# The opening of a two-block kernel: the first tile turned as loaded, its norm row as a column, the first weights by halves

## The chip, the cores and the metric

The kernel runs on one core of a Trainium2 chip. A core has a matrix engine (TensorE, "PE" in the profile), VectorE (DVE), ScalarE (ACT), GpSimd (POOL) and SyncE (SP), each with its own instruction stream; they wait for each other on semaphores. Transfers from HBM are asked for by an engine's queue (SP and ACT here by hardware queues, POOL by a software one) and moved by 16 DMA engines. The metric is the device time of one launch in microseconds, the median of several.

## The reference

Two transformer blocks of two layers each, on 256 tokens of width 1024, in float32. The change touches only how the first layer starts:

```python
for i in range(DEPTH):
    h = rms_norm(x, norm_mix_pre[i])
    z = h @ w_in[i]
    c_q, c_kv, k_rope, q_c, k_c, v_c, g_a, g_b, g_c = jnp.split(z, split_points, axis=-1)
    ...

def rms_norm(x, gain):
    y = x * lax.rsqrt(jnp.mean(x * x, axis=-1, keepdims=True) + RMS_EPS)
    return y * gain
```

The scale of a token (the rsqrt) is a factor of its row and can be applied behind the product with the weights; the gain is a factor of a column of `x` and has to be applied ahead of it. Positions of the tokens feed a rotation of some columns and a mask by distance for windowed attention.

## The kernel before

**Tiles.** The 256 tokens are two tiles of 128 rows: `xs[:, 0]` (x0) and `xs[:, 1]` (x1). A matmul needs the activations with the width on the partitions, so each tile is multiplied by its gain row into `ht` (VectorE, "h" in the profile), turned by TensorE against `ident` in two groups of four 128x128 blocks into PSUM banks 2 and 3, and copied out.

**Two parts.** Each factor is kept as a high part rounded to the fast matmul type and a low part, the rest. ScalarE makes `act_hi` from the turned tile and `whi` from the loaded weights `raw`; VectorE makes `act_lo` and `wlo` by subtraction. A product is three passes: high rows by high weights (L571), low rows by high weights (L565), high rows by low weights (L556).

**Units.** The weights stream through three slots in units of up to 128x2048 words (1 MB), each loaded by two transfers. SyncE asks for unit u as soon as the low part of unit u - 3 is made. The first product takes its 512 columns from units 0 and 1 (tile 0, then tile 1), the second from units 2 and 3. A product of a unit with one tile is 12 matmuls of 512 columns. `stay_warm(n)` is n turns of `ident` whose result nobody reads; at the start 18 of them stand behind the turns of tile 0.

**Order.** All is written by hand, engine by engine, and every engine does its instructions in order. In the opening ScalarE first asks for the gain row (broadcast to all partitions), the positions (`posk` along the free axis for all partitions, `posq` down the partitions) and the rotation tables. It squares x0, makes `act_hi`, then the halves of unit 0 (`first_split`, counted by `s_first_hi` and `hi`), asks for x1, and does the halves of unit 1. VectorE has the gain product of tile 0, `act_lo`, the low parts of both units, the gain product of tile 1, then the work on positions (6 steps, `PART_STEPS`) and distances (8 more) for `mask`, then `act_lo` of tile 1 and the low part of unit 2. GpSimd makes constants, the inverse root of tile 0, and a table of angles from `posq`. TensorE turns tile 1 in the middle of the pass by low weights of unit 1. Then each engine enters the loop over the two layers, whose body begins with the first product; `Ready` holds what a product waits for at the seam. Semaphores named in `counted` are raised to `BASE` by TensorE at the start.

## Time and profile before

| | us |
|---|---|
| median of 3 runs (1907.06 to 1907.66) | 1907.35 |
| span of the profiled execution | 1904.2 |
| around the span, if that execution took the median time | 3.15 |
| TensorE busy | 1868.7 |
| VectorE, ScalarE, GpSimd busy | 1107.1, 958.9, 150.4 |
| first product's first matmul begins | 13.03 |
| unit 3's first matmul begins | 29.84 |

The profiler shows the span, from the first to the last instruction; no time of its own is given for that execution beside it, so the median stands for it. Times of the opening are counted from the span's start. A timeline row is a run of like instructions: start, time from the first's start to the last's end, how many, and in brackets how long the engine had stood idle and what released it. Ends of matmuls are modelled and overlap with the next, so starts are to be compared.

### The profile page before, as it was taken

To read this page: it belongs to the slowest core of one execution; us is meant where nothing else is said; L and a number is where in the kernel's file an instruction comes from. 1 tells how busy PE (TensorE), PEld (TensorE's weight loads), DVE (VectorE), ACT (ScalarE), POOL (GpSimd) and SP (SyncE) were. 2 spreads that over 40 slices of the span, in tenths; PEclk is the share of its full clock that TensorE was granted. 3 is DMA by queue.
4 is the path that set the end of the run, shared out by engine and by line. 5 is a ranking of instruction groups with operands and counts; after the bars stand their busy time and mean duration, and the time that the engine had idled before them with its cause. 6 is when DMAs were issued, how large, how long until landed. Compare 5 with 4: busy or idle time off the path is not lost.

```text
span 1904.2 us, 26150 instructions
## 1 busy us (share of the span) xinstructions
PE 1868.7 (98%) x8988; PEld 1523.3 (80%) x8988; DVE 1107.1 (58%) x1365; ACT 958.9 (50%) x1277; POOL 150.4 (8%) x259
## 2 busy tenths in 40 slices
PE   8999999999999999999999999999999999999998
PEld 7777888887877888888788887788888888868887
DVE  6666565448676575446754456655465445575454
ACT  5664454445675464445544446644454444564443
POOL 5210010001300010000100012000011000100000
PEclk9999999999999999999999999999999999999999
DMA  6335565554524546565655554455565564526553
GB/s 225 123 119 184 179 217 190 178 183 151 166 90 166 205 164 204 193 198 177 201 190 178 179 202 141 143 195 179 182 219 170 184 198 169 195 90 197 178 178 107
DMA packets 204987, 332.72 MB, mean 175 GB/s; under 512 B 11360, under 2 KB 150240, under 8 KB 204896
## 3 DMA queue, kind: packets, MB, share of 16 engines
q1 hardware_dynamic: 200240, 319.08, 49.9%
q0 software_dynamic: 3120, 11.02, 1.7%
q10 hardware_dynamic: 1536, 1.47, 0.2%
q8 instruction: 50, 0.82, 0.2%
q14 instruction: 41, 0.34, 0.1%
HBM read 330.48 MB, written 1.05 MB: 174 GB/s over the span
## 4 chain that ended last, share of the span: by engine, by line
PE 88%; issue 4%; DVE 3%; ACT 3%; DMA 1%; POOL 0%; DVEq 0%; SPq 0%; POOLq 0%; ACTq 0%
PE ps L571 27%; PE ps L565 27%; PE ps L556 27%; PE ps L598 3%; ACT whi L1254 1%; PE ps L771 1%; PE ps L759 1%; PE ps L787 1%; ACT prob L1352 1%; DVE wlo L1738 1%; DMA raw<-w_in_dram 0%; DVE prob L1878 0%; DMA xs<-x_dram 0%; DVE prob L1851 0%; DVE act_lo L1744 0%
## 5 line engine op out<-in xcount | busy, mean ns | idle before, releaser
L1738 DVE TENSOR_TENSOR wlo<-raw,whi 128x2048 fp32r<-128x2048 f32 (+1 forms) x306 | 690.6, 2257 | 510.3 <-ACT whi L1254 509.8
L1254 ACT ACTIVATE whi<-raw 128x2048 fp32r<-128x2048 f32 (+1 forms) x306 | 576.9, 1885 | 422.4 <-PE ps L565 422.3
L571 PE MATMUL ps<-whi,act_hi 128*128 128x512 f32 (+2 forms) x1632 | 442.0, 392 | 5.1 <-issue 2.4
L556 PE MATMUL ps<-wlo,act_hi 128*128 128x512 f32 (+2 forms) x1632 | 438.7, 387 | 0.0
L565 PE MATMUL ps<-whi,act_lo 128*128 128x512 f32 (+2 forms) x1632 | 432.2, 386 | 1.5 <-DVE act_lo L1744 1.5
L565 PEld LDWEIGHTS ps<-whi,act_lo 128*128 128x128 f32 x1632 | 303.9, 188 | 64.4 <-DVE act_lo L1744 2.3
L556 PEld LDWEIGHTS ps<-wlo,act_hi 128*128 128x128 f32 x1632 | 302.2, 188 | 61.8 <-issue 1.1
L571 PEld LDWEIGHTS ps<-whi,act_hi 128*128 128x128 f32 x1632 | 297.5, 188 | 64.1 <-issue 2.8
L1299 ACT ACTIVATE hid<-ps,stat 128x256 f32<-128x256 f32 x132 | 62.6, 474 | 282.9 <-PE ps L598 197.4
L2320 POOL TENSOR_TENSOR stat<-stat,eps 128x1 f32<-128x1 f32 x43 | 22.4, 521 | 1471.4 <-ACT prob L1286 1471.1
L1791 DVE SCALAR_TENSOR_TENSOR hid<-ps,stat,hid 128x256 f32<-128x256 f32 x132 | 63.6, 482 | 123.7 <-ACT hid L1299 123.7
L571 PE MATMUL ps<-whi,hid_hi 128*128 128x512 f32 x496 | 133.2, 390 | 0.0
L556 PE MATMUL ps<-wlo,hid_hi 128*128 128x512 f32 x496 | 133.1, 390 | 0.0
L565 PE MATMUL ps<-whi,hid_lo 128*128 128x512 f32 x496 | 132.6, 389 | 0.0
L565 PEld LDWEIGHTS ps<-whi,hid_lo 128*128 128x128 f32 x496 | 93.1, 188 | 19.3
L556 PEld LDWEIGHTS ps<-wlo,hid_hi 128*128 128x128 f32 x496 | 93.0, 188 | 19.3
L571 PEld LDWEIGHTS ps<-whi,hid_hi 128*128 128x128 f32 x496 | 92.7, 188 | 18.9
L1352 ACT ACTIVATE prob<-prob,soft 128x128 f32<-128x128 f32 (+1 forms) x96 | 44.3, 464 | 12.1 <-DVE soft L1851 12.1
L1261 ACT ACTIVATE act_hi<-ps 128x512 fp32r<-128x512 f32 x56 | 30.5, 594 | 37.9 <-PE ps L598 37.8
L1744 DVE TENSOR_TENSOR act_lo<-ps,act_hi 128x512 fp32r<-128x512 f32 x56 | 36.4, 684 | 21.3 <-ACT act_hi L1261 21.3
L771 PE MATMUL ps<-ident,prob 128*128 128x128 f32 x224 | 37.8, 285 | 10.1 <-DVE prob L1878 8.7
L771 PEld LDWEIGHTS ps<-ident,prob 128*128 128x128 f32 x224 | 24.1, 140 | 27.8 <-DVE prob L1878 11.8
(217 smaller groups left out, 1611.5 us busy)
## 6 DMA issues: line engine op xcount, KB each, us to landing
raw<-ffn_w_gate_dram SPq DMA_DIRECT2D x88, 512.0 KB, 4.0
raw<-ffn_w_up_dram SPq DMA_DIRECT2D x88, 512.0 KB, 5.0
raw<-ffn_w_down_dram SPq DMA_DIRECT2D x88, 512.0 KB, 3.9
raw<-w_in_dram SPq DMA_DIRECT2D x64, 512.0 KB, 4.4
raw<-w_ffn_gate_dram SPq DMA_DIRECT2D x44, 512.0 KB, 4.0
raw<-w_ffn_up_dram SPq DMA_DIRECT2D x44, 512.0 KB, 5.0
raw<-w_ffn_down_dram SPq DMA_DIRECT2D x44, 512.0 KB, 3.9
raw<-a_w_qkv_dram SPq DMA_DIRECT2D x24, 512.0 KB, 4.5
```

Source lines behind the costliest of these rows:

```text
L556: last = nc.tensor.matmul(o, hi, a, start=False, stop=last_pass and stop and i == len(parts) - 1)
L565: last = nc.tensor.matmul(o, lo, a, start=False, stop=last_pass and stop and i == len(parts) - 1)
L571: nc.tensor.matmul(o, hi, a, start=start and i == 0, stop=False)
L598: last = nc.tensor.transpose(bank[0:rows, j * P:(j + 1) * P], src(j), ident[:, :])
L771: last = nc.tensor.transpose(ps[:, bank, kt * S + t * P:kt * S + (t + 1) * P], prob[:, sc % PROBS, t, kt * P:(kt + 1) * P], ident[:, :])
L1254: nc.scalar.activation(whi[:, u % SLOTS, 0:words], raw[:, u % SLOTS, 0:words], ACT.Copy)\
L1261: nc.scalar.activation(dst, ps[:, 2 + k % 2, 0:n * P].rearrange("p (j c) -> p j c", j=n), ACT.Copy).then_inc(sem("turn_hi"), 1)
L1299: nc.scalar.activation(hid[:, t, :], ps[:, t, 0:CH], ACT.Silu, scale=scale_of(w, norm + t))\
L1352: last = nc.scalar.activation(prob[:, i % PROBS, t, 0:cols], src, ACT.Exp, bias=nm[:, t:t + 1], scale=scale or (-1.0 if causal else 1.0), ...
L1738: nc.vector.tensor_tensor(wlo[:, u % SLOTS, 0:words], raw[:, u % SLOTS, 0:words], whi[:, u % SLOTS, 0:words].bitcast(F32), ALU.subtract)\
L1744: return nc.vector.tensor_tensor(dst, src, hi.bitcast(F32), ALU.subtract)
L1791: nc.vector.scalar_tensor_tensor(hid[:, t, :], ps[:, t, CH:2 * CH], scale_of(w, norm + t), hid[:, t, :], ALU.mult, ALU.mult).then_inc(sem( ...
```

## The change

The turn of tile 0 no longer waits for the gain. TensorE turns x0 as it lies; VectorE multiplies the turned groups (PSUM to `ht`) by the gain as a column, `first_col`, a new input laid out by the host with one column of eight words on each partition; ScalarE and VectorE make `act_hi` and `act_lo` from `ht`. For tile 1 the gain row is needed on all partitions: it is now loaded to one partition (4 KB) and spread by two matmuls with a row of ones into PSUM banks 0 and 1, from where VectorE reads it. The ident turns behind it go from 18 to 4, in bank 7. ScalarE asks for x1 ahead of unit 0's split and for `posk` behind it. The first two units are taken by halves in every layer: TensorE begins with the first half's two matmuls when `first_hi` says so. VectorE's order changes: gain product of tile 1 ahead of unit 1's low part; `act_lo` of tile 1 and unit 2's low part ahead of the distances. The counters are raised half by TensorE, half by VectorE. GpSimd's table waits for `posq` and the table of frequencies alone.

```diff
-WARM_SHORT, WARM_LONG, WARM_START = 6, 3, 18
+WARM_SHORT, WARM_LONG, WARM_START = 6, 3, 4
...
+        one_row = hid[0:1, 1, 0:P]
+        first_gain = gains[0:1, 0, :]
...
                 if t == 0:
-                    if ready.seam:
+                    if by_halves:
+                        pe.wait_ge(sem("first_hi"), w.at("first_hi", u + 1))
+                    elif ready.seam:
                         unit_hi_there(u)
...
-            for s in counted:
+            for s in counted[0::2]:
                 pe.sem_inc(s, BASE)
             pe.wait_ge(s_ident, 2)
             w.layer = 0
-            rows(TN_MIX, "h_ready", 0)[1](0)
-            stay_warm(WARM_START)
+            pe.wait_ge(s_in["x0"], 16)
+            for g in range(2):
+                turn(TN_MIX + g, lambda j: xs[:, 0, (4 * g + j) * P:(4 * g + j + 1) * P], 4, bank=2 + g)
+            pe.wait_ge(s_in["gain"], 16)
+            for n in range(2):
+                last = nc.tensor.matmul(ps[:, n, :], one_row, first_gain[:, n * 512:(n + 1) * 512],
+                                        start=True, stop=True)
+            last.then_inc(s_row, 1)
+            stay_warm(WARM_START, 7)
...
-            act.dma_start(gains[:, 0, :], A["gains"][0:1, :].partition_broadcast(P).rearrange("p a n -> p (a n)"))\
-                .then_inc(s_in["gain"], 16)
-            act.dma_start(posk[:, :], A["positions"][0:1, :].partition_broadcast(P).rearrange("p a n -> p (a n)")).then_inc(s_in["pos"], 16)
+            act.dma_start(first_col[:, :], A["first_col"][:, :]).then_inc(s_col, 16)
+            act.dma_start(first_gain, A["gains"][0:1, :]).then_inc(s_in["gain"], 16)
...
             square(0, xs[:, 0, :])
-            turned_rows_hi(TN_MIX, (0,))
...
-            first_split(0)
+            for g, (there, n) in enumerate(((s_turned, 1), (sem("h_ready"), w.at("h_ready", 1)))):
+                act.wait_ge(there, n)
+                nc.scalar.activation(act_hi[:, 4 * g:4 * g + 4, 0:P],
+                                     ht[:, 0, g * 512:(g + 1) * 512].rearrange("p (j c) -> p j c", j=4),
+                                     ACT.Copy).then_inc(sem("turn_hi"), 1)
             act.dma_start(xs[:, 1, :], A["x"][0, P:S, :]).then_inc(s_in["x1"], 16)
-            first_split(1)
+
+            split(1, True)
+            act.dma_start(posk[:, :], A["positions"][0:1, :].partition_broadcast(P).rearrange("p a n -> p (a n)")).then_inc(s_posk, 16)
+            split(1, True)
...
-            dve.wait_ge(s_in["gain"], 16)
-            dve.wait_ge(s_in["x0"], 16)
-            nc.vector.tensor_tensor(ht[:, 0, :], xs[:, 0, :], gains[:, 0, :], ALU.mult).then_inc(sem("h_ready"), 1)
-            turned_rows_lo(TN_MIX, 0)
+            for s in counted[1::2]:
+                dve.sem_inc(s, BASE)
+            dve.wait_ge(s_col, 16)
+            first = [ht[:, 0, g * 512:(g + 1) * 512].rearrange("p (j c) -> p j c", j=4) for g in range(2)]
+            for g, done_part in enumerate((s_turned, sem("h_ready"))):
+                dve.wait_ge(sem("turn_done"), w.at("turn_done", TN_MIX + g + 1))
+                cols = first_col[:, 4 * g:4 * g + 4].unsqueeze(2).to_broadcast([P, 4, P])
+                nc.vector.tensor_tensor(first[g], ps[:, 2 + g, :].rearrange("p (j c) -> p j c", j=4), cols, ALU.mult)\
+                    .then_inc(done_part, 1)
...
+            first_lo(0)
+            dve.wait_ge(s_row, 1)
             dve.wait_ge(s_in["x1"], 16)
-            nc.vector.tensor_tensor(ht[:, 1, :], xs[:, 1, :], gains[:, 0, :], ALU.mult).then_inc(sem("h_ready"), 1)
+            first_row = ps[:, 0:2, :].rearrange("p b n -> p (b n)")
+            nc.vector.tensor_tensor(ht[:, 1, :], xs[:, 1, :], first_row, ALU.mult).then_inc(sem("h_ready"), 1)
+            first_lo(1)
...
+            turned_rows_lo(TN_MIX, 1)
+            split(1)
             dve.wait_ge(s_parts, n_parts[0])
             for t in range(T):
...
-            turned_rows_lo(TN_MIX, 1)
-            split(1)
             with dve.Fori(0, DEPTH) as li:
```

VectorE, from the low parts of units 0 and 1 to the first steps on positions. Before (`first_hi` and `hi` are ScalarE's counts of halves, `h` is `ht`):

```order
L2137 TENSOR_TENSOR wlo<-raw,whi 128x1024 [waits first_hi]
L2137 TENSOR_TENSOR wlo<-raw,whi 128x1024 [waits hi]
L2137 TENSOR_TENSOR wlo<-raw,whi 128x1024 [waits first_hi]
L2137 TENSOR_TENSOR wlo<-raw,whi 128x1024 [waits hi]
L2142 TENSOR_TENSOR h<-xs,gains 128x1024 [waits in_x1]
L2152 TENSOR_SCALAR alibi<-posk 128x256 [waits in_pos]
L2153 TENSOR_SCALAR alibi<-posk 128x256
```

After:

```order
L2169 TENSOR_TENSOR wlo<-raw,whi 128x1024 [waits first_hi]
L2169 TENSOR_TENSOR wlo<-raw,whi 128x1024 [waits hi]
L2178 TENSOR_TENSOR h<-xs,ps 128x1024 [waits in_x1,first_row]
L2169 TENSOR_TENSOR wlo<-raw,whi 128x1024 [waits first_hi]
L2169 TENSOR_TENSOR wlo<-raw,whi 128x1024 [waits hi]
L2190 TENSOR_SCALAR alibi<-posk 128x256 [waits posk_in,in_pos]
L2191 TENSOR_SCALAR alibi<-posk 128x256
```

The gain product of tile 1, with its wait for x1, has moved ahead of both halves of unit 1.

VectorE, from the last steps on positions to the loop (`mask` and `alibi` hold the distances, `act_lo` is of tile 1, the `wlo` of 2048 columns is unit 2's). Before:

```order
L2156 CAST posf<-posi 128x4
L2160 TENSOR_SCALAR mask<-probT,posf 128x256 [waits parts]
L2162 TENSOR_SCALAR alibi<-probT,posf 128x256
L2160 TENSOR_SCALAR mask<-probT,posf 128x256
L2162 TENSOR_SCALAR alibi<-probT,posf 128x256
L2165 TENSOR_TENSOR alibi<-alibi,mask 128x256 [waits parts]
L2165 TENSOR_TENSOR alibi<-alibi,mask 128x256
L2168 SCALAR_TENSOR_TENSOR mask<-alibi 128x256 [waits parts]
L2168 SCALAR_TENSOR_TENSOR mask<-alibi 128x256
L1744 TENSOR_TENSOR act_lo<-ps,act_hi 128x4x128 [waits turn_hi] x2
L1738 TENSOR_TENSOR wlo<-raw,whi 128x2048 [waits hi]
L2173 UNCONDITIONAL_BRANCH
```

After:

```order
L2194 CAST posf<-posi 128x4
L1766 TENSOR_TENSOR act_lo<-ps,act_hi 128x4x128 [waits turn_hi] x2
L1760 TENSOR_TENSOR wlo<-raw,whi 128x2048 [waits hi]
L2200 TENSOR_SCALAR mask<-probT,posf 128x256 [waits parts]
L2202 TENSOR_SCALAR alibi<-probT,posf 128x256
L2200 TENSOR_SCALAR mask<-probT,posf 128x256
L2202 TENSOR_SCALAR alibi<-probT,posf 128x256
L2205 TENSOR_TENSOR alibi<-alibi,mask 128x256 [waits parts]
L2205 TENSOR_TENSOR alibi<-alibi,mask 128x256
L2208 SCALAR_TENSOR_TENSOR mask<-alibi 128x256 [waits parts]
L2208 SCALAR_TENSOR_TENSOR mask<-alibi 128x256
L2211 UNCONDITIONAL_BRANCH
```

The two `act_lo` and unit 2's `wlo` have moved ahead of the eight steps on distances, which now stand right before the loop.

TensorE, from the turn of tile 0 to the end of unit 0's product with it (L605 and L616 are the ident turns). Before:

```order
L598 MATMUL ps<-ident,h 128x128 [waits turn_read_v,h_ready,ident_ready]
L598 MATMUL ps<-ident,h 128x128 x3
L598 MATMUL ps<-ident,h 128x128 [waits turn_read_v]
L598 MATMUL ps<-ident,h 128x128 x3
L605 MATMUL ps<-ident 128x128 x18
L1046 UNCONDITIONAL_BRANCH
L1046 ISA
L541 ISA [waits half_read_a]
L545 ISA [waits hi]
L571 MATMUL ps<-whi,act_hi 128x512 [waits turn_hi]
L571 MATMUL ps<-whi,act_hi 128x512 x3
```

After:

```order
L609 MATMUL ps<-ident,xs 128x128 [waits in_x0,ident_ready]
L609 MATMUL ps<-ident,xs 128x128 x7
L1061 MATMUL ps<-gains,hid 128x512 [waits in_gain]
L1061 MATMUL ps<-gains,hid 128x512
L616 MATMUL ps<-ident 128x128 x4
L1065 UNCONDITIONAL_BRANCH
L1065 ISA
L592 ISA [waits half_read_a]
L551 ISA [waits first_hi]
L579 MATMUL ps<-whi,act_hi 128x512 [waits turn_hi]
L579 MATMUL ps<-whi,act_hi 128x512
L547 ISA
```

The turns read `xs`, two matmuls for the gain row stand in the place of 14 ident turns, and the first product waits for `first_hi`, which counts halves.

## Rows read from the trace of the kernel before

**Rows 1.** Page, part 1: engine, busy us (share of span) x instructions.

```profile
PE 1868.7 (98%) x8988; PEld 1523.3 (80%) x8988; DVE 1107.1 (58%) x1365; ACT 958.9 (50%) x1277; POOL 150.4 (8%) x259
```

**Rows 2.** Chain of waits, 8 to 31 us: start us, us, what.

```profile
2.21 8.65 DMA raw<-w_in_dram
...
10.89 6.50 DMA xs<-x_dram
...
17.42 1.23 DVE h L2142
```

**Rows 3.** Timeline of TensorE: start, busy us, line, operation, count [idle before].

```profile
7.56 1.94 PE L598 MATMUL ps<-ident,h 128*128 128x128 f32 x8 [7.56 <-DVE h L2131]
9.29 4.05 PE L605 MATMUL ps<-ident 128*128 128x128 f32 x18
13.03 1.31 PE L571 MATMUL ps<-whi,act_hi 128*128 128x512 f32 x4
...
18.70 1.10 PE L598 MATMUL ps<-ident,h 128*128 128x128 f32 x8 [0.19 <-DVE h L2142]
...
23.36 1.20 PE L565 MATMUL ps<-whi,act_lo 128*128 128x512 f32 x4 [1.13 <-DVE act_lo L1744]
...
27.12 1.07 PE L571 MATMUL ps<-whi,act_hi 128*128 128x512 f32 x4
...
29.84 1.07 PE L571 MATMUL ps<-whi,act_hi 128*128 128x512 f32 x4
...
62.40 1.13 PE L759 MATMUL ps<-kT,qT 96*128 96x256 f32 x4
```

**Rows 4.** Timeline of ScalarE, the opening.

```profile
10.89 1.06 ACT L1567 ACTIVATE whi<-raw 128x1024 fp32r<-128x1024 f32 x1 [0.75 <-DMA raw<-w_in_dram]
...
19.45 1.09 ACT L1261 ACTIVATE act_hi<-ps 128x512 fp32r<-128x512 f32 x2 [3.63 <-PE ps L598]
20.43 1.92 ACT L1254 ACTIVATE whi<-raw 128x2048 fp32r<-128x2048 f32 x1
```

**Rows 5.** Timeline of VectorE, the opening.

```profile
14.91 2.42 DVE L2137 TENSOR_TENSOR wlo<-raw,whi 128x1024 fp32r<-128x1024 f32 x2 [0.56 <-ACT whi L1567]
...
18.56 0.34 DVE L2152 TENSOR_SCALAR alibi<-posk 128x256 int32<-128x256 int32 x1
...
19.91 0.38 DVE L2160 TENSOR_SCALAR mask<-probT,posf 128x256 f32<-128x256 f32 x1
...
22.62 1.27 DVE L1744 TENSOR_TENSOR act_lo<-ps,act_hi 128x512 fp32r<-128x512 f32 x2
...
26.02 0.74 DVE L1925 TENSOR_SCALAR zs<-ps,stat 128x512 f32<-128x512 f32 x1
26.68 2.27 DVE L1738 TENSOR_TENSOR wlo<-raw,whi 128x2048 fp32r<-128x2048 f32 x1
...
36.04 1.35 DVE L1738 TENSOR_TENSOR wlo<-raw,whi 128x1152 fp32r<-128x1152 f32 x1
```

**Rows 6.** DMA queues 0:14.5 (q1 SyncE, q10 ScalarE); x0's transfer; q10 13:14.4; q10 14.5:17.

```profile
q1 hardware_dynamic: 1647, 3.44, 67.6%
q10 hardware_dynamic: 1248, 0.68, 17.6%
...
xs<-x_dram SPq DMA_DIRECT2D x1, 512.0 KB, 5.1
...
q10 hardware_dynamic: 1, 0.00, 0.1%
...
q10 hardware_dynamic: 144, 0.52, 53.6%
```

**Rows 7.** Stretches: us, busy (x) of five engines, PE clock, DMA share, GB/s.

```profile
4.00:5.00 1.00, 0.00 (x0) 0.00 (x0) 0.00 (x0) 0.98 (x1) 0.00 (x0) 1.00 0.95 307
9.50:12.50 3.00, 3.00 (x16) 3.00 (x16) 1.72 (x3) 2.21 (x3) 1.42 (x5) 1.00 1.05 373
```

**Rows 8.** Timeline of TensorE at the seam of the two layers.

```profile
464.79 1.18 PE L571 MATMUL ps<-whi,act_hi 128*128 128x512 f32 x4 [2.38 <-issue]
```

57 lines of the change are left out of this document (36 added, 21 removed).

## The prediction

> **What bounds the kernel now.** First the page: TensorE is busy 98% of the span [rows 1], so over most of the program only a shorter TensorE stream could pay, and the change shortens none. What it can move is the opening, until TensorE has its first unbroken run of work. So I read next the chain of waits of the opening [rows 2]. The reader is to see that no engine stands in its first 17 us, but transfers do: the weights' first unit until 10.86 us, then x's second tile, asked for at 10.89 and landed at 17.40, then VectorE's product with the norm row (17.42) and its integer and distance work. TensorE's rows [rows 3] show the same from the other side: it turns tile 0 at 7.56, fills with 18 turns of ident, begins the first product at 13.03, turns tile 1 at 18.70, stands 1.13 us before 23.36 for act_lo, and then runs without a gap; unit 3's first matmul is at 29.84. I take that 29.84 as the mark: what moves it moves the end. ScalarE's rows [rows 4] and VectorE's [rows 5] say what stands ahead of it. VectorE is the engine without air: from 14.91 to the end of unit 3's low part at 28.95 it has no gap worth the name, while TensorE needs that low part only at 29.84, a slack of 0.9 us.
>
> The sum is made against the span of 1904.2 us; the three times have a median of 1907.35, so 3.15 us lie around the span, which nothing here touches.
>
> **The first tile and its weights.** Removed from the front of ScalarE's queue: the norm row broadcast to 128 partitions (0.52 MB) and the key positions (0.13 MB, now behind the first weight unit). In their place come a column of 4 KB and one row of 4 KB. Before 14.5 us the two hardware queues moved 3.44 and 0.68 MB [rows 6]; nearly all of the 0.68 is what leaves. At the 307 GB/s of 4 to 5 us [rows 7] 0.65 MB are 2.1 us; at the 373 of 9.5 to 12.5 [rows 7] they are 1.7, and I take the stretch in which the row itself moved. Unit 0 therefore lands near 10.86 - 2.1 = 8.8 and x0, 5.1 us on its way [rows 6] and landed just before 6, near 4.4. ScalarE's square runs as soon as its table is in. Turn of tile 0: eight turns at 213 ns (18 in 4.05 us with their tail, [rows 3]) end near 6.2. The two VectorE products by the column are not in the trace; the nearest rows are act_lo's, 1.27 us for two [rows 5], and 1.23 for the whole row product removed [rows 2]: equal, taken as 0.65 each. ScalarE makes its two act_hi in 1.09 [rows 4], done by about 7.9, and then asks for x1, 3.0 us sooner than now.
>
> The two row matmuls (1 partition, 512 columns, plain f32) are new. The nearest row is a pair of f32 matmuls of 256 columns, 1.13 us, in four records [rows 3]: twice the columns gives some 2.1 us for the pair, 4.2 at half the rate. Between 6.2 and about 10.4 at the latest they and the 4 ident turns are done. First half of unit 0: 8.8 + 1.06 [rows 4] = 9.9. So the first product begins near 10.4 where it began at 13.03: a **lead of 2.6 us on TensorE**. The halves of later layers (one more ACTIVATE for two units of each layer: twice 1.06 for 1.92 [rows 4], four times 0.2 us) fall in ScalarE time with slack: at the seam of the layers TensorE stands 2.38 us on "issue", for no engine [rows 8]; if that were gone the 0.2 would show. The extra wait on TensorE there I put at 0.05, between 0 and 0.1 for each layer. The 45 counters on two engines cost nothing while both wait for x0, and up to 1 us if they did not.
>
> **What becomes of the lead.** VectorE's order is the point. Before: unit 0's low part, unit 1's, row product of tile 1, positions, distances, act_lo of tile 1, unit 2's. After: unit 0's low part, *wait for x1*, row product, unit 1's low part, positions, act_lo, unit 2's, distances, then the loop with unit 3's. So the wait for x1 has unit 1's low part queued behind it, and TensorE waits for that in the middle of unit 1's first product; and the distances, which cost TensorE 1.13 us before 23.36, now stand ahead of unit 3's low part, whose slack was 0.9.
>
> When does x1 land? Before, it was asked for at 10.89, and ScalarE's queue moved nothing from 13.0 to 14.4 (1 packet) and all of its 0.52 MB from 14.5 on [rows 6]. It was not late for want of turns: once it had packets it had half the engines. Its transfer came out only when SyncE's six transfers, all issued before it, were nearly through: 3.44 of 3.67 MB. I read that as one line of waiting for both queues. Asking 3 us sooner then brings nothing by itself; x1 begins when SyncE's queue stands at 3.44 MB, that is 14.5 - 2.1 = 12.4, and **lands at X = 17.4 - 2.1 = 15.3**.
>
> From X on, by rows: row product 1.23 [rows 2] to X+1.25; unit 1's low part 2.42 [rows 5] to X+3.65; on TensorE two matmuls (0.45) and the turn; act_hi starts 0.75 after the turn (18.70 to 19.45, [rows 3, 4]) at X+4.85; unit 2's high part ends 2.9 later (19.45 to 22.35, [rows 4]) at X+7.75. VectorE has done positions (1.3, 18.56 to 19.91, [rows 5]) and act_lo (1.27) by X+6.75 and waits 1 us for that high part, which it never did before. Then unit 2's low part, as large as unit 3's, 2.27 to X+10.05, distances 2.7 (19.91 to 22.62, [rows 5]) to X+12.75, zs 0.66 (26.02 to 26.68), unit 3's low part 2.27 [rows 5] to X+15.7. TensorE could be there at X+14.1 (its turn at X+4.1, then as before from 18.70 to 29.84 less the wait of 1.13 [rows 3]). So unit 3 begins at X+15.75. With X = 15.3 that is 31.05 against 29.84: **1.2 us later**. Even is X = 14.1. The whole lead lies in TensorE's wait for unit 1's low part, about 3.9 us long. Behind it there is air: unit 4's low part ends at 37.4 [rows 5] where it is wanted three products of 2.72 (27.12 to 29.84, [rows 3]) after unit 3's start, at 38.0; and the norm constants ahead of it come from GpSimd, which gets its positions sooner. So the 1.2 passes to the end.
>
> Sum: 1907.35 + 1.2 + 0.05 = **1908.6**. With x1 between 14.8 and 15.9 it is 1908.1 to 1909.2.
>
> **The clock.** The 18 ident turns and the first matmul ran at the lower level: 213 ns a turn against 137 with their tail for the eight at 18.70 [rows 3], although the granted clock reads 1.00 in that stretch [rows 7]; the rate doubled near 13.4, 5.9 us after TensorE's first work. The Trainium skill, "TensorE: Matmul & The Clock Gate", section on the HAM clock gate, says the half rate is the default, lifted by sustained activity and brought back by idleness; by that rule 4 turns in place of 18 would leave the first products at half rate. In the sum this costs nothing, since 20 matmuls at half rate lose 4.3 us in front of a wait that is otherwise 3.9 us long. But the wait itself is longer than any gap the trace shows TensorE to come out of at full rate (2.38 us, [rows 8]).
>
> **Rivals.** (1) *x1 comes soon after it is asked for.* ScalarE's queue is served in turn, and the quiet from 13.0 to 14.4 was something else. Then X = 7.9 + 5.1 (x0's own time, [rows 6]) = 13.0, unit 3 begins at 28.75, and the time is 1906.3; with X at 12.4 or 14.1 it is 1905.7 or 1907.4. The Trainium skill, "DMA: Bandwidth & Descriptors", section on queues, rings and completion order, states this rule: each engine takes the queues it has work for in turn. The silence of the one queue for 1.4 us speaks against it, the wide share it then had for it.
> (2) *The clock falls in the wait for unit 1's low part* (slower). TensorE idles from 15.1 (10.4 + 2.72 + two thirds of 2.72, and 0.2 for unit 1's second half) to 19.0 and comes back at 1.2 GHz: the two matmuls and four turns before act_hi take 0.9 us more, and if the low rate held as long as it did at the start (5.8 us), 2.9 us are lost of the 1.65 that TensorE has to spare. Unit 3 then begins 0.9 to 1.25 later: 1909.5 to 1909.9. It decides if the gap is longer than TensorE can idle at full rate, which is somewhere above 2.4 us. To pass 0.2% it needs x1 at 17 too; that gives 1911.2.
> (3) *The change does not do what it says:* the first weights land no sooner, because the broadcast row was not what held them. Then X = 17.4, unit 3 at 33.15, and 1910.7. Against it stands that the DMA engines were 95% busy from 4 to 5 us [rows 7], half with these bytes.
> (4) *The lead survives.* If x1 did land before unit 0's low part is done (12.3) unit 3 would begin at 28.1: 1905.6. No more than that can be had, for VectorE's own work from there is 15.7 us long.
>
> **How the numbers follow.** Forecast 45%, rival 1 27%, rival 2 12%, rival 3 6%, rival 4 5%, other 5%. Within 0.2% (3.8 us, about what a measurement of this kernel can tell from no change) lie all of them but the tails: faster by more 5%, same 91%, slower by more 4%. The range from 1905.3 to 1910.2 takes in the forecast, rivals 1, 2 and 4, and leaves out 3 and the tails.
>
> **What would show it.** Right: first product near 10.4; a TensorE gap of 3 to 4 us ahead of L562 (wlo) in unit 1, which ends with VectorE's low part; x1 landing near 15.3; a second, new gap ahead of unit 3's first matmul, released by VectorE's wlo, at about 31.0; VectorE waiting about 1 us for unit 2's whi. Wrong: x1 landing at 13 or before, matmul spacing of 0.43 us after 19 us, unit 0 landing after 10, or no gap at unit 3.

## The result, and the profile after

| | before | after |
|---|---|---|
| median, us (21 runs each, same chip) | 1907.17 | 1910.21 |
| lowest to highest, us | 1905.54 to 1909.54 | 1908.20 to 1910.90 |
| ratio after to before, with 95% interval | | 1.0015 (1.0008 to 1.0021) |
| span of the profiled execution, us | 1904.2 | 1908.8 |
| unit 3's first matmul begins | 29.84 | 30.50 |

The changed kernel is 3.0 us slower, 0.15%. The forecast was 1.2 us slower. The time stands at the very upper end of its range (1910.2). Only 0.66 us of the 3.0 lie where the prediction looked for them, in the opening. The other 2.4 come from something that it never priced.

The page's first part reads as before [rows 1], but TensorE is busy 5.6 us longer with ten records fewer:

```profile
PE 1874.3 (98%) x8978; PEld 1523.3 (80%) x8978; DVE 1107.1 (58%) x1366; ACT 959.6 (50%) x1281; POOL 147.2 (8%) x260
```

The chain of waits from 4.6 to 18.4 us (start, duration, what) answers to [rows 2]:

```profile
4.59 1.96 PE ps L609 x8
...
6.57 0.70 DVE h L2158
...
7.30 7.46 DMA xs<-x_dram
...
14.85 1.09 DVE h L2178
...
15.99 2.37 DVE wlo L2169 x2
```

The chain shows that x1 is still the piece that all wait for. It is asked for 3.6 us sooner than before (7.30 against 10.89) and lands 2.6 us sooner. It takes 7.46 us where it took 6.50.

TensorE's timeline (start, busy us, line, operation, count, idle time before and its releaser), which answers to [rows 3]; L579 is whi by act_hi, L571 whi by act_lo, L562 wlo by act_hi, L609 the turns, L1061 the row product, L616 the turns of ident:

```profile
6.46 3.78 PE L1061 MATMUL ps<-gains,hid 1*128 1x512 f32 x4
10.17 1.11 PE L616 MATMUL ps<-ident 128*128 128x128 f32 x4
10.94 2.06 PE L579 MATMUL ps<-whi,act_hi 128*128 128x512 f32 x4
12.79 1.44 PE L571 MATMUL ps<-whi,act_lo 128*128 128x512 f32 x4
...
18.41 0.73 PE L562 MATMUL ps<-wlo,act_hi 128*128 128x512 f32 x2 [1.46 <-DVE wlo L2169]
...
30.50 1.20 PE L579 MATMUL ps<-whi,act_hi 128*128 128x512 f32 x4 [1.72 <-DVE wlo L1760]
```

ScalarE's and VectorE's timelines, which answer to [rows 4, 5]:

```profile
8.84 1.06 ACT L1276 ACTIVATE whi<-raw 128x1024 fp32r<-128x1024 f32 x1 [0.91 <-DMA raw<-w_in_dram]
```

```profile
14.85 1.22 DVE L2178 TENSOR_TENSOR h<-xs,ps 128x1024 f32<-128x1024 f32 x1 [2.56 <-DMA xs<-x_dram]
15.99 2.36 DVE L2169 TENSOR_TENSOR wlo<-raw,whi 128x1024 fp32r<-128x1024 f32 x2
...
20.30 1.29 DVE L1766 TENSOR_TENSOR act_lo<-ps,act_hi 128x512 fp32r<-128x512 f32 x2 [0.79 <-ACT act_hi L1285]
22.59 2.35 DVE L1760 TENSOR_TENSOR wlo<-raw,whi 128x2048 fp32r<-128x2048 f32 x1 [1.00 <-ACT whi L1278]
24.86 0.34 DVE L2200 TENSOR_SCALAR mask<-probT,posf 128x256 f32<-128x256 f32 x1
...
27.50 0.75 DVE L1947 TENSOR_SCALAR zs<-ps,stat 128x512 f32<-128x512 f32 x1
28.16 2.28 DVE L1760 TENSOR_TENSOR wlo<-raw,whi 128x2048 fp32r<-128x2048 f32 x1
```

Here is the mechanism that was forecast: VectorE waits 2.56 us for x1 with unit 1's low part queued behind that wait, TensorE stands for it (1.46 us at 18.41), VectorE waits 1.00 us for unit 2's high part, then the distances (24.86 to 27.5) stand ahead of unit 3's low part, and TensorE waits 1.72 us for that.

**Past the opening.** Laid beside each other, the starts of the same matmuls in the two traces do not keep their distance of 0.66 us. After is 1.3 us behind at 459 us. It gains nothing on before, and loses nothing to it, in the stretches in which the feed-forward products run (220 to 460, 700 to 1100 us). It falls back in those whose products have `four_hi`, `co_hi`, `oc_hi` and their like as operands. The groups of TensorE instructions from 130 to 220 us, shapes kept apart (count, busy us, mean ns of one), before:

```profile
L556 PE MATMUL ps<-wlo,act_hi 128*128 128x512 f32 x64 | 17.4, 391 | 0.0
...
L565 PE MATMUL ps<-whi,four_lo 128*128 128x512 f32 x24 | 6.5, 392 | 0.0
...
L571 PE MATMUL ps<-whi,co_hi 128*128 128x512 f32 x16 | 4.3, 392 | 0.0
```

and after:

```profile
L562 PE MATMUL ps<-wlo,act_hi 128*128 128x512 f32 x64 | 17.4, 391 | 0.0
...
L571 PE MATMUL ps<-whi,four_lo 128*128 128x512 f32 x24 | 6.6, 395 | 0.0
...
L579 PE MATMUL ps<-whi,co_hi 128*128 128x512 f32 x16 | 4.4, 395 | 0.0
```

A matmul with `act_hi` takes 391 ns in both. One with `four_lo` or `co_hi` takes 395 where it took 392. Three nanoseconds are little, but a matmul's mean holds the tail that overlaps the next one (a group of four takes 1.07 us, so they start some 227 ns apart), and there are some hundreds of them. `act_hi` is declared ahead of the new tensor `first_col`, the others behind it. `first_col` has 8 words, 32 bytes, on each partition, and moves all that is declared behind it by 32 bytes. That became the first theory to test.

**The seam.** In the profiled execution of after the granted clock fell once on the way, 1.3 us after TensorE had come out of the gap between the two layers (466.22). Stretches of all engines, whose third number from the end is TensorE's granted clock, of after, and of before for the first of them:

```profile
440.00:480.00 40.00, 37.33 (x171) 30.03 (x169) 32.88 (x27) 21.09 (x23) 6.61 (x10) 0.96 0.43 136
...
468.00:470.00 2.00, 2.00 (x7) 1.54 (x6) 1.70 (x2) 0.33 (x1) 0.27 (x1) 0.50 0.01 4
```

```profile
440.00:480.00 40.00, 37.20 (x177) 29.90 (x175) 34.62 (x28) 22.25 (x25) 6.17 (x9) 1.00 0.49 157
```

0.50 is the lower of its two levels, 1.2 GHz. TensorE's groups there took 1.91 us instead of 1.07, and the fall costs about 1.65 us. It is not the change's doing.

The times of most kernels here fall into a sooner and a later kind, mostly 1.4 to 2.1 us apart, and in the kernel before the mean granted clock tells them apart: of 33 executions, 20 had 0.998 and took 1906.96 to 1908.03 us, 13 had 0.999 and a median of 1905.7 (one of them took 1908.39). In e1, e2 and e5 to e11 the profiled execution has this fall and is one of the later kind; e4's has none and is of the sooner. Only e12, below, does not fit. The profile of before has no fall, that of after has one. So the spans (1904.2 and 1908.8) differ by 4.6 us and the medians by 3.0. A median of eleven times can land in either kind. So below, where two medians lie in different kinds, the kinds' own medians are compared ("kind against kind"). For before and after these are 2.8 and 3.1 us apart, as the medians say. The profiled execution of after took 1910.45 us with a span of 1908.8, so 1.65 us lie around the span, not 3.15; over all executions it is 1.7.

### The profile page after: what moved, and what is told of

It reads as the page before. It is cut to its first block, busy times and chain, and to the rows that moved or that the text cites. A ratio compares the mean times of both kernels' runs of the same rounds, so it can differ in the third digit from the quotient of the medians.

```text
span 1908.8 us, 26140 instructions
## 1 busy us (share of the span) xinstructions
PE 1874.3 (98%) x8978; PEld 1523.3 (80%) x8978; DVE 1107.1 (58%) x1366; ACT 959.6 (50%) x1281; POOL 147.2 (8%) x260
## 4 chain that ended last, share of the span: by engine, by line
PE 88%; issue 4%; DVE 4%; ACT 3%; DMA 1%; POOL 0%; DVEq 0%; POOLq 0%; ACTq 0%
PE ps L579 27%; PE ps L562 27%; PE ps L571 27%; PE ps L609 4%; ACT whi L1278 1%; PE ps L782 1%; PE ps L770 1%; PE ps L798 1%; DVE wlo L1760 1%; ACT prob L1376 1%; DMA xs<-x_dram 1%; DVE prob L1900 0%; DVE prob L1873 0%; ACT act_hi L1285 0%; DVE soft L1897 0%
## 5 line engine op out<-in xcount | busy, mean ns | idle before, releaser
L1278 ACT ACTIVATE whi<-raw 128x2048 fp32r<-128x2048 f32 (+2 forms) x308 | 575.6, 1869 | 421.2 <-PE ps L571 421.1
L579 PE MATMUL ps<-whi,act_hi 128*128 128x512 f32 (+2 forms) x1632 | 443.0, 392 | 6.9 <-issue 2.5
L562 PE MATMUL ps<-wlo,act_hi 128*128 128x512 f32 (+2 forms) x1632 | 439.7, 388 | 1.5 <-DVE wlo L2169 1.5
L571 PE MATMUL ps<-whi,act_lo 128*128 128x512 f32 (+2 forms) x1632 | 433.0, 386 | 0.4 <-DVE act_lo L1766 0.4
L571 PEld LDWEIGHTS ps<-whi,act_lo 128*128 128x128 f32 x1632 | 304.6, 188 | 63.2 <-DVE act_lo L1766 0.8
L562 PEld LDWEIGHTS ps<-wlo,act_hi 128*128 128x128 f32 x1632 | 302.7, 188 | 63.8 <-DVE wlo L2169 1.9
L579 PEld LDWEIGHTS ps<-whi,act_hi 128*128 128x128 f32 x1632 | 298.3, 189 | 66.3 <-DVE wlo L1760 3.1
L579 PE MATMUL ps<-whi,hid_hi 128*128 128x512 f32 x496 | 133.2, 390 | 0.0
L562 PE MATMUL ps<-wlo,hid_hi 128*128 128x512 f32 x496 | 133.1, 390 | 0.0
L571 PE MATMUL ps<-whi,hid_lo 128*128 128x512 f32 x496 | 132.6, 389 | 0.0
L571 PEld LDWEIGHTS ps<-whi,hid_lo 128*128 128x128 f32 x496 | 93.1, 188 | 19.3
L562 PEld LDWEIGHTS ps<-wlo,hid_hi 128*128 128x128 f32 x496 | 93.0, 188 | 19.3
L579 PEld LDWEIGHTS ps<-whi,hid_hi 128*128 128x128 f32 x496 | 92.7, 188 | 18.9
L1766 DVE TENSOR_TENSOR hid_lo<-ps,hid_hi 128x256 fp32r<-128x256 f32 x124 | 46.3, 415 | 0.0
```

The costliest lines, as they stand in the source:

```text
L562: last = nc.tensor.matmul(o, hi, a, start=False, stop=last_pass and stop and i == len(parts) - 1)
L571: last = nc.tensor.matmul(o, lo, a, start=False, stop=last_pass and stop and i == len(parts) - 1)
L579: nc.tensor.matmul(o, hi, a, start=start and i == 0, stop=False)
L1278: nc.scalar.activation(whi[:, u % SLOTS, half:words], raw[:, u % SLOTS, half:words], ACT.Copy)\
L1766: return nc.vector.tensor_tensor(dst, src, hi.bitcast(F32), ALU.subtract)
```

## The experiments

Each was compared with the kernel before on the same chip: 1907.15 us for e1 to e4, 1907.2 for e5 to e8, 1907.36 for e9 and e10, 1906.08 for e11 and e12. That last one is the same kernel with more executions of the sooner kind among its 21, so the ratios, not differences across chips, are compared there.

### Is it the 32 bytes? (e1, e2, e7, e8)

e1, the kernel before and nothing but an unused tensor:

```diff
         cs2 = sb("cs2", [P, 2, T, ROT // 2])
+        unused = sb("unused", [P, DT])
```

> The kernel before with one unused tensor of 32 bytes a partition in the place where the change puts its column; no instruction differs. Theory (placement): half of the 3 us that the change costs is not in the opening. In the trace of after the lead or lag against before is +0.66 us at unit 3 but grows in the stretches whose products read tensors that lie behind the new column (from 130 to 220 us, 600 to 665 us and in the second block) and not in the feed-forward stretches, whose operands lie ahead of it. Then this kernel is 1.3 to 2.2 us slower than before, with unit 3's first matmul still at 29.84 and the lag growing in the same stretches. Rival (the program itself: more waits, other counters): the same time as before within 0.3 us.

Measured: 1909.49 us, ratio 1.0012 (1.0003 to 1.0021), so **+2.3 us for a tensor that nobody touches** (kind against kind 2.4). That is a little more than the theory gave. Unit 3's first matmul stood at 30.03, 0.2 later than before, though nothing ahead of it is changed: so much the opening differs from one execution to the next (e7, below, has 29.70).

e2, the changed kernel, with the column padded to 64 bytes:

```diff
-        first_col = sb("first_col", [P, DT])
+        first_col = sb("first_col", [P, 2 * DT])[:, 0:DT]
```

> The kernel after with its column tensor padded to 64 bytes a partition, so that all tensors behind it move by 64 bytes and not by 32. Theory (placement, and 64 bytes is the grain): 1.3 to 2.2 us faster than after, so 0.7 to 1.6 us slower than before. If any shift hurts: as after, 2.9 us slower than before. Rival (the program itself): as after.

Measured: 1906.04 us, ratio 0.9996 (0.9986 to 1.0005), equal to the kernel before. The median lies 4.2 us under the changed kernel's, but it is of the sooner kind and the changed kernel's of the later; kind against kind it is 3.1 us, and so are the spans of the two profiled executions (1905.7 and 1908.8), both with the fall at the seam. That is more than the 2.3 or 2.4 that e1 costs. So 64 bytes were not merely harmless, and two more sizes were put to the kernel before, with `3 * DT` and `2 * DT` words in the place of `DT`:

> The kernel before with an unused tensor of 64 bytes per partition behind the small trig table, everything behind it shifted by 64 bytes. Nothing else is changed, nothing is left out. Theory (only the odd multiple of 32 bytes costs): as the kernel before, 1906.7 to 1907.7, and the pace of the matmul groups at 130 to 220 us as in the kernel before. Rival (any shift costs, because what mattered were certain absolute places of the tensors): 1908.7 to 1910.0, as with 32 bytes.

> The kernel before with an unused tensor of 96 bytes per partition at the same place. Nothing else is changed, nothing is left out. Theory (operands that begin at an odd multiple of 32 bytes cost): 2.0 to 2.6 us above the kernel before, 1908.9 to 1910.0, like e1. Rival (it was the 32-byte size or its particular place): 1906.7 to 1907.7.

Measured: 64 bytes 1905.31 us, ratio 0.9992 (0.9983 to 1.0001); 96 bytes 1909.04, ratio 1.0013 (1.0004 to 1.0022). The odd multiples of 32 cost 1.8 and 2.3 us. 64 bytes seem to give back about 1 us (kind against kind 1.0 and 1.2; the medians' 1.9 again compare two kinds). Its interval just reaches 1, but its groups say the same. From 130 to 220 us, of the kernel before with 64 bytes, then with 96:

```profile
L557 PE MATMUL ps<-wlo,act_hi 128*128 128x512 f32 x64 | 17.4, 391 | 0.0
...
L566 PE MATMUL ps<-whi,four_lo 128*128 128x512 f32 x24 | 6.4, 389 | 0.0
...
L572 PE MATMUL ps<-whi,co_hi 128*128 128x512 f32 x16 | 4.3, 389 | 0.0
```

```profile
L566 PE MATMUL ps<-whi,four_lo 128*128 128x512 f32 x24 | 6.6, 396 | 0.0
...
L572 PE MATMUL ps<-whi,co_hi 128*128 128x512 f32 x16 | 4.4, 395 | 0.0
```

In the built programs `four_hi` begins at these bytes of its partition (`co_hi` 16384 further on, so with the same remainder):

```
kernel              four_hi begins at   rest by 128   co_hi, mean ns   median us
before              156480              64            392              1907.2
before + 32         156512              96            395              1909.49
before + 64         156544               0            389              1905.31
before + 96         156576              32            395              1909.04
after               156512              96            395              1910.21
after, column 64    156544               0            389              1906.04
```

For the products with `co_hi` and `four_lo` there are three levels, set by where the operand begins: a multiple of 128 bytes 389 ns, of 64 only 392, of 32 only 395 or 396. `four_hi` by `wlo` shows two (391 at the first two, 395 at the last). `act_hi`, whose place (106624, a multiple of 128) none of these edits moves, keeps its 390 or 391 in all of them. This explains both surprises: after fell from the middle level to the worst, and e2 rose to the best. From best to worst it is 2.9 us by the spans of the profiled executions of e7 and e8 (1904.5 and 1907.4), each with the fall at the seam, and 2.9 and 3.0 kind against kind. The opening's price by itself, both kernels at the best level (e2 against e7), is 0.7 us by the medians and 0.9 and 1.1 kind against kind, and unit 3 starts at 30.71 and 29.70; the traces of before and after say 0.66. So the opening costs 0.7 to 1.0. That the place of what is declared behind the column is the cause is shown. Why the hardware cares was not looked into.

### The order on VectorE (e3, e6, e5, e9)

e3, the changed kernel with unit 1's low part ahead of the wait for x1:

```diff
             first_lo(0)
+            first_lo(1)
             dve.wait_ge(s_row, 1)
...
-            first_lo(1)
```

> The kernel after with one thing undone on VectorE: unit 1's low part stands ahead of the wait for x1 and the row product of tile 1 again. Theory (VectorE's time from x1 on sets unit 3): in the trace of after VectorE stands 2.56 us for x1 (14.85) with unit 1's low part behind it. Here that part is done by 15.3, the row product by 16.5, and unit 3's first matmul comes at 28.2 (after: 30.50), so the time is 2.3 us below after's, 0.6 us above before's. Rival (TensorE's late turn or x1 itself sets it): unit 3 moves by less than 0.5 us.

Measured: 1909.32 us, ratio 1.0012 (1.0003 to 1.0021). TensorE's rows around unit 3, and the stretches behind:

```profile
28.59 1.21 PE L579 MATMUL ps<-whi,act_hi 128*128 128x512 f32 x4 [1.84 <-DVE wlo L1760]
...
31.05 1.91 PE L571 MATMUL ps<-whi,act_lo 128*128 128x512 f32 x4
32.76 1.38 PE L579 MATMUL ps<-whi,act_hi 128*128 128x512 f32 x4
```

```profile
30.00:33.00 3.00, 3.00 (x9) 2.33 (x8) 0.90 (x3) 2.82 (x6) 2.51 (x7) 0.50 0.55 191
```

Unit 3 came 1.9 us sooner, where the theory had 2.3, and then 1.6 of them were gone: the granted clock went to 0.50, some 1.4 us after the 1.84 us in which TensorE waited for unit 3's low part. From 60 us to the seam this trace is 0.2 us ahead of the changed kernel's. The changed kernel came out of a wait of 1.72 us at the same place without a fall (31.53 with 1.07). So the order's worth was real, and the wait that VectorE left in place cost it again by way of the clock, in this execution; of e3's other ten, only one (1907.54) stands clear of the rest.

e6 puts only the distances back to where the kernel before has them, ahead of tile 1's act_lo:

```diff
-            turned_rows_lo(TN_MIX, 1)
-            split(1)
             dve.wait_ge(s_parts, n_parts[0])
             ...
             assert n_parts[0] == DISTANCE_STEPS
+            turned_rows_lo(TN_MIX, 1)
+            split(1)
```

> The changed kernel with one of its moves undone: the distances stand ahead of act_lo of tile 1 and of unit 2's low part, as in the kernel before. Nothing is left out. Theory: in the changed kernel VectorE waited 0.79 us for act_hi and 1.00 us for unit 2's high part and did the 2.7 us of distances behind them; ahead of them they lie in those waits, so unit 3's first matmul comes at 28.6 to 29.2 instead of 30.50, TensorE waits under 0.6 us ahead of it, and with the 32-byte shift still in place the time is 1908.2 to 1909.0 (1.3 to 1.9 us below the changed kernel's). Rival: TensorE then waits for act_lo of tile 1 (it would end near 23.4 instead of 21.6) and gets back no more than 0.3 us at unit 3, 30.2 or later, and the time stays at 1909.8 to 1910.5.

Measured: 1907.58 us, ratio 1.0007 (0.9998 to 1.0016), with the 32-byte shift still in it: 2.6 us under the changed kernel in the medians. Unit 3's first matmul came at 29.79 with no wait ahead of it, not at 28.6 to 29.2: TensorE waited 0.62 us for act_lo of tile 1 instead, and from there it was bound by its own work. Nearer to the theory than to the rival, with a smaller shift (0.7 us) than either unit 3 or the medians had been given. The trace of e6 is 1.1 us ahead of the changed kernel's from 31 us to the end. The rest of the medians' 2.6 is the kinds of execution: 7 of e6's 11 were of the sooner kind (1907.0 to 1908.2), 8 of the changed kernel's 21 (1908.2 to 1909.1), and kind against kind it is 1.2 and 1.5 us.

e5 takes all together: the padded column, e3's order, e6's order, and the small trig table asked for behind the positions (e4, below).

> The changed kernel with four things at once: the column tensor is padded from 32 to 64 bytes per partition, unit 1's low part stands ahead of x1's wait and of the second tile's row product on VectorE, the distances stand ahead of act_lo of tile 1 again (the order of the kernel before), and ScalarE asks for the small trig table behind the positions. Nothing is left out. Theory: the terms add. Of e2 (1906.04, first matmul of unit 3 at 30.71) the order of the two products of VectorE gives 1.9 us sooner at unit 3 (28.59 in e3), the distances fill the 0.9 and 1.0 us in which VectorE waited for ScalarE there (about 1.9 us more), and the small table 0.5: first matmul of unit 3 at 26.3 to 27.0 with under 0.7 us of wait ahead of it, the granted clock stays at 2.4 GHz behind it, and the time is 1902.0 to 1903.5, 3.7 to 5.2 us under the kernel before. Rival 1 (the lead is given back): later in the opening TensorE waits for a unit's landing or for the table's z-half, which do not move with VectorE, and of some 4 us at unit 3 less than 1 us is left at 60 us: 1905.0 to 1906.0. Rival 2: the clock falls anyway within a few microseconds of unit 3, and 1.4 us go: 1903.5 to 1905.0, with matmul groups of 1.6 and 1.9 us between 27 and 33.

Measured: **1904.57 us, ratio 0.9986 (0.9977 to 0.9995)**, faster than both kernels. TensorE's rows:

```profile
21.23 1.19 PE L571 MATMUL ps<-whi,act_lo 128*128 128x512 f32 x4 [0.69 <-DVE act_lo L1766]
...
27.71 1.07 PE L579 MATMUL ps<-whi,act_hi 128*128 128x512 f32 x4
```

Unit 3 starts 3.0 us sooner than in e2, without a wait and with no fall of the clock there, and the two traces keep 2.6 to 2.8 us between them to the end (kind against kind 2.4 and 2.8; the medians show 1.5, e2's being of the sooner kind). The seam has its fall in both. So rival 1 (given back later) and rival 2 fell. The theory was 1 us too hopeful: it counted VectorE's air only, and TensorE's own work from 10.99 to 27.71, plus 0.69 us for act_lo, ends later than VectorE is ready (26.8).

e9 takes away the four turns of ident ahead of the first product and puts half the distances behind unit 2's low part:

```diff
-WARM_SHORT, WARM_LONG, WARM_START = 6, 3, 4
+WARM_SHORT, WARM_LONG, WARM_START = 6, 3, 0
```

> e5 with two edits more: no identity turns behind the row product in the opening (4 before), and of the distances the last four operations (add and maximum, 1.6 us) behind unit 2's low part instead of ahead of act_lo of tile 1. Nothing is left out. Theory: in e5 TensorE's first product (10.99) followed the identity turns although unit 0's half had been there since about 9.9, and act_lo of tile 1 was 0.69 us late; now the first product comes at 10.1 to 10.3, act_lo of tile 1 is in time, and unit 3's first matmul comes at 26.7 to 27.1 instead of 27.71, so 0.6 to 1.0 us under e5: 1903.4 to 1904.1. Rival 1 (the pace of the first products is half until about 13 whatever stands ahead, and leaving the turns out moves that moment later): the first product comes at 10.2, but the rate rises no earlier than 13.5, unit 1's first product stays within 0.3 us of 14.8, and the time is e5's, 1904.3 to 1905.0. Rival 2: VectorE's low parts of units 2 and 3 become late instead, with over 0.5 us of wait ahead of unit 3, and nothing is left of it.

Measured: **1903.24 us, ratio 0.9982 (0.9973 to 0.9991)**, the lowest median. But not for the reason given. The first product did come at 10.18, and yet:

```profile
10.18 2.08 PE L579 MATMUL ps<-whi,act_hi 128*128 128x512 f32 x4
12.05 1.91 PE L571 MATMUL ps<-whi,act_lo 128*128 128x512 f32 x4
13.76 1.91 PE L562 MATMUL ps<-wlo,act_hi 128*128 128x512 f32 x4
15.47 1.39 PE L579 MATMUL ps<-whi,act_hi 128*128 128x512 f32 x4
...
28.48 1.20 PE L579 MATMUL ps<-whi,act_hi 128*128 128x512 f32 x4 [0.58 <-DVE wlo L1760]
```

At half the pace a matmul starts 0.43 us after the one before it, at the full one 0.23; by the starts above the pace rose only near 16.1, where it rose near 13.1 in e5. Unit 1's first product came at 15.47, and unit 3's low part was 0.58 late: rival 2 and, in its late pace, rival 1. In the trace e9 is 0.6 us *behind* e5. But the missing turns need not be what delayed the pace. In e2 TensorE does the same as in the changed kernel up to there, four turns included, and yet:

```profile
14.56 1.65 PE L562 MATMUL ps<-wlo,act_hi 128*128 128x512 f32 x4
16.05 1.09 PE L579 MATMUL ps<-whi,act_hi 128*128 128x512 f32 x4
```

The pace rose near 15.8 there, near 14.8 in e6 and near 12.9 in e3. With 18 turns it differs too: they took 4.05 us in before and 2.73 in e7. So the moment moves by up to 2.9 us between executions of one opening, and one trace of each cannot tell what the turns do. e9's two kinds of execution have the same times as e5's (1902.5 to 1903.3 and 1904.8 to 1905.7, against 1902.6 to 1903.3 and 1904.4 to 1905.6), only 7 of 11 were of the sooner kind instead of 4; the lower median is that count. Which of e5 and e9 is better is not settled.

### x1's transfer (e4)

e4, the changed kernel with the small trig table (512 pieces of 32 bytes) asked for behind the positions instead of ahead of x1:

```diff
-            act.dma_start(cs2[:, :, :, :], A["trig2"]...).then_inc(s_in["const"], 16)
...
             act.dma_start(posk[:, :], A["positions"]...).then_inc(s_posk, 16)
+            act.dma_start(cs2[:, :, :, :], A["trig2"]...).then_inc(s_in["const"], 16)
```

> The kernel after with the rotation table of the second block (512 pieces of 32 bytes) asked for behind x1 and the key positions instead of ahead of them. It asks why x1 takes 7.5 us from its issue at 7.30. Theory A (x1 waits behind ScalarE's own small pieces, one a turn): its packets begin near 9.3 instead of 10.7, it lands near 12.6 instead of 14.81, unit 3 begins near 28.3, 2.2 us below after. Theory B (one line for both queues, as in the prediction): x1 begins when SyncE's six transfers are handed out, landing at 14.5 to 15.3, no change. Theory C (bandwidth: x1 has only its share beside SyncE's queue): landing 0.3 to 0.8 us sooner.

Measured: 1909.39 us, ratio 1.0012 (1.0003 to 1.0021). x1 landed 0.8 us sooner after a request at the same time, and unit 3 came 0.7 us sooner:

```profile
7.28 6.71 DMA xs<-x_dram
```

```profile
29.80 1.20 PE L579 MATMUL ps<-whi,act_hi 128*128 128x512 f32 x4 [1.73 <-DVE wlo L1760]
```

What x1 is late for is read from the queues (packets, MB, share of the 16 engines; q1 is SyncE's, q10 ScalarE's). The changed kernel from 0 to 10.5 us, then from 10.5 to 14:

```profile
q1 hardware_dynamic: 1203, 2.58, 68.7%
q10 hardware_dynamic: 925, 0.03, 5.1%
```

```profile
q1 hardware_dynamic: 391, 0.75, 59.1%
q10 hardware_dynamic: 386, 0.59, 47.3%
```

x1's bytes began to move between 10.5 and 10.7, when SyncE's queue stood at 2.6 MB and not at the 3.44 of [rows 6], and the two queues moved packets in nearly equal numbers. So there is no one line for both queues, and theory B falls. What the small pieces do is seen from 10.5 to 12 alone, first the changed kernel, then e4:

```profile
q10 hardware_dynamic: 209, 0.17, 36.3%
```

```profile
q10 hardware_dynamic: 82, 0.34, 56.5%
```

x1 began at 10.7 in e4 too, where its queue had moved 0.00 MB from 8.5 to 10.3 and no packet from 9.5 on. So some 3.4 us passed after the request with many small pieces ahead or few, and theory A falls. But in the changed kernel 32-byte pieces of the trig table still took turns of that queue, and x1 got half the bytes. Theory C's term (x1 has only its share) is right and as large as the upper end of what was given for it, 0.8 us. The turns are not simply one packet each, though: without the small pieces e4's queue moved 82 packets where SyncE's moved 148, and 0.34 MB where SyncE's moved 0.29.

### The clock at the seam and in the opening (e10, e11, e12)

e10 is e9 without the six turns of ident at the end of the layer loop.

```diff
-WARM_SHORT, WARM_LONG, WARM_START = 6, 3, 0
+WARM_SHORT, WARM_LONG, WARM_START = 0, 3, 0
```

> e9 without the six identity turns that stand at the end of the layer loop's body (TensorE did them in 0.8 us just ahead of the gap between the layers). Nothing is left out. Theory A (the gap of 2.2 us ends a fixed time after the loop's branch): the first product of the second layer comes 0.6 to 0.8 us sooner against e9, the gap stays at 2.1 to 2.5 us. Theory B (the gap ends by something that the turns do not move, the fetch of the loop's start having been asked for earlier): the first product comes at the same time within 0.2 us, and the gap reads 2.9 to 3.2 us. Under either the granted clock still falls behind the gap in most executions (two kinds of times 1.6 to 1.7 us apart): the theory on the clock is that it falls behind a gap of this length in some executions and not in others; if the gap of B makes it longer, the sooner kind of times gets rarer.

Measured: 1905.31 us, ratio 0.9989 (0.9980 to 0.9998). TensorE behind the gap:

```profile
463.29 2.07 PE L579 MATMUL ps<-whi,act_hi 128*128 128x512 f32 x4 [3.21 <-issue]
```

In e9 that group begins at 463.04 behind a gap of 2.24. So it is theory B: the gap's end moves by 0.25 us and not by 0.8, and the turns fill 0.8 us of it for nothing. The sooner kind of execution got rarer, 2 of 11 (1902.23 and 1902.89) against 7 of 11 in e9. That is the direction that a longer gap should give; with 11 executions each it is a hint, not a proof. The sooner kind's times are e9's, so the turns cost no time and may buy the clock.

e11 and e12 are e5 and e9 with ten turns of ident ahead of x0's wait:

```diff
             pe.wait_ge(s_ident, 2)
             w.layer = 0
+            stay_warm(10, 7)
             pe.wait_ge(s_in["x0"], 16)
```

> e5 with ten identity turns more on TensorE at its very start, from the identity's readiness at about 2.1 us, where TensorE had nothing to do until x's first tile landed at 4.6. Nothing is left out. What is asked: what raises TensorE's pace in the opening (in e5 matmuls took half the pace until about 13.1, in e9, without the four identity turns behind the row product, until about 15.8). Theory (busy time of whatever kind ahead counts): the ten turns, 2.3 us, bring the rise of the pace forward by 1.5 us or more, to 11.5 or sooner; unit 0's products then end 0.7 to 1.0 us sooner, unit 3's first matmul comes at 26.8 to 27.2 instead of 27.71, if VectorE's low parts are there by then (unit 3's ended at 26.8 in e5), and the time is 1903.6 to 1904.0. Rival (what counts is only what stands between the row product and the first product, the row product itself having one row of 128): the pace rises at 13.1 as in e5, unit 3 at 27.7, time 1904.3 to 1904.9.

> e9 with the same ten identity turns at TensorE's start. Nothing is left out. Theory of e11 (busy time of whatever kind ahead counts): the pace rises by 13.5 or sooner instead of 15.8 and unit 1's first product comes at 14.0 or sooner instead of 15.47. Rival (only what stands right ahead of the first product counts): the pace rises at 15.5 to 16.0 as in e9, and unit 1's first product comes at 15.3 to 15.6. The whole time is bound by VectorE's low part of unit 3 (0.58 us late in e9), which does not move: 1903.2 to 1904.2 under either.

Measured: 1903.94, ratio 0.9987 (0.9978 to 0.9996), and 1903.53, ratio 0.9982 (0.9973 to 0.9991). Both expectations rest on a wrong premise. TensorE, of e11:

```profile
4.10 2.37 PE L616 MATMUL ps<-ident 128*128 128x128 f32 x10 [4.10 <-issue]
6.26 1.91 PE L609 MATMUL ps<-ident,xs 128*128 128x128 f32 x8
...
16.14 1.19 PE L562 MATMUL ps<-wlo,act_hi 128*128 128x512 f32 x4
```

TensorE did not start at 2.1 but at 4.10, released by nothing that the profile shows, so the ten turns pushed x0's turns from 4.6 to 6.3 and all of TensorE's opening by 1.6 us. In these traces the pace rose near 16.3 (e12: 16.6), later than in e5 (13.1) and e9 (16.1), and e11 is 1.0 us behind e5. The medians show no such loss: the ratios are e5's and e9's. The profiled executions are not typical: e11's took 1905.58, the slowest of eleven, and e12's 1904.52, one of the three slowest. In e12 even the clock's mean is the other way round: 0.999 in those three, which took 1904.5 to 1905.1, and 0.998 in the eight that took 1902.6 to 1903.8. In the eight the ten turns may have helped; no trace of one was taken. What decides when the pace rises in the opening **stays open**.

## Why the prediction was right and where it was wrong

**The total** ended at the range's upper end, and its sign and verdict (within 0.2%) were right. Its composition was not, and that the range reached it is luck: most of the 3.0 came from a term that it did not have. Medians: +3.0 = 0.7 (opening, trace) + 2.3 (32-byte shift, e1). The 0.05 put on the seam is not shown: the gap there reads 2.50 us in after and 2.38 in [rows 8], but 2.18 in e2, which has the change, and 2.14 to 2.22 in e1, e7 and e8, which do not.

**The step that failed: new operations were priced, a new tensor was not.** The part on the edits costs every instruction and transfer of `first_col`, and nothing for its 32 bytes in front of the operands of half the program. No row of the trace of before could have given 2.3 us. But the rows could have set a bound: TensorE is 98% busy with equal matmuls, so one nanosecond on each of its some 8900 is 9 us, and the declaration moves every tensor behind it. The forecast of 1.2 was twice the opening's 0.66, and that error covered 0.6 of the missing 2.3.

**First weights, x0, first half of unit 0.** Forecast 8.8, 4.4, 9.9; measured 8.84, 4.45, 9.90. Taking the broadcast row's bytes at the rate of the stretch in which they moved was right.

**TensorE's first product.** Forecast 10.4, measured 10.94. The row product took 3.78 us where 2.1 to 4.2 had been given: the slow end. The column products of VectorE took 0.70 as priced.

**x1's landing.** Forecast X = 15.3, measured 14.76; the size nearly right, the reason wrong. "One line of waiting for both queues" predicts that x1 starts when SyncE's queue stands at 3.44 MB; it stood at 2.58. (The 3.67 MB are x0 and the six transfers of weights, seven in all.) Rival 1 had the mechanism (the queue is served in turn, as the Trainium skill, "DMA: Bandwidth & Descriptors", section on queues, rings and completion order, has it; the 391 and 386 packets above agree, e4's 148 and 82 agree only in that both queues moved at once). It took x0's 5.1 us for x1's transfer; beside a full queue of SyncE's, and with the trig table's small pieces in its own, it took 7.46. The quiet of ScalarE's queue before 14.4 [rows 6] was the end of the 3.6 us between the request at 10.89 and the first packets; it is 3.4 in after. The prediction saw the silence and read waiting into it.

**From X to unit 3.** Forecast X + 15.75; measured 30.50 - 14.76 = 15.74. Every step of that sum stood: act_hi of tile 1 at X + 4.9, VectorE's wait for unit 2's high part of 1.00 us, the distances ahead of unit 3. With the true X the forecast would have been 0.67 late, and 0.66 was measured.

**TensorE's wait for unit 1's low part.** Forecast 3.9 us, measured 1.46, since the first product began 0.5 later, its first matmuls ran at half the pace until about 13.6, and X was 0.5 sooner. It cost nothing, because the end was set by VectorE. Rival 2 did not occur there: TensorE came out of 1.46 us at the full pace.

**The clock.** "Longer than any gap the trace shows TensorE to come out of at full rate (2.38 us)" took one execution for the rule. In the profiles of after, e2 and e9 the granted clock fell behind a gap of 2.50, 2.18 and 2.24 us at the seam, and in e3 also behind 1.84, while e12 came out of 2.18 and e4 out of 2.71 at the full pace. So rival 2's condition, a gap longer than 2.4 us, was not the right one. The gap decides together with something else that differs between executions, which no run here names. The Trainium skill, "TensorE: Matmul & The Clock Gate", section on the HAM clock gate, has idleness bring the half rate back; the runs agree with that.

**Around the span.** 3.15 us were taken from a span and a median that belong to two kinds of execution; it is 1.7.

## What to carry to other kernels

A new small tensor is an edit to the address of everything declared behind it. Give it a size that keeps the matmul operands on multiples of 128 bytes, or declare it last, and compare one group's mean nanoseconds before looking for waits: here that was worth 2.3 us, and the whole opening 0.7 to 1.0. When times fall into two kinds, look at which kind each median is of before subtracting them. When a wait moves, look at what is queued behind it on the same engine (unit 1's low part, 1.9 us at unit 3) and close the gaps that remain, since TensorE may come out of the next one at half its clock.

## What the runs showed of the hardware that was not expected

- A matmul of 128x512 with `co_hi` takes 389, 392 or 395 ns in the profile by whether `co_hi` begins at a multiple of 128, of 64 or only of 32 bytes. With all that is declared behind the column moved alike, it is 2.9 us of this kernel's 1907 between best and worst (e7 and e8).
- The granted clock fell to 1.2 GHz behind gaps of 1.84 to 3.21 us in some executions, at a loss of 1.6 to 1.7 us each time (after, e3); before came out of 2.38, e12 of 2.18 and e4 of 2.71 us without a fall.
- In the opening the full pace began between 12.9 and 15.8 us in six executions (after, e2 to e6) in which TensorE does the same up to there.
- TensorE did not start before 4.10 us (e11) and 4.11 (e12) into the span, though the identity that it waited for was made by 2.06. What it did until then, its part of the counters included, the profile does not show.
- Some 3.4 to 3.6 us pass between ScalarE's request for x1 and its first bytes, with its queue nearly empty (e4) as well as not. Then the two queues share the engines, and 32-byte pieces in x1's queue take turns from it: 0.17 against 0.34 MB in 1.5 us.
